# Updating the states of sample units in row tiles of TensorE

## Chip, cores and metric

One core of one Trainium2 chip runs the whole program. The metric is the time of one launch on the device, in microseconds (us).

## The reference, cut to what matters

The program computes one layer of a decoder for a prompt of 2048 tokens and for a group of 8 short sample sequences of 8 tokens each. One of its three parts is an mLSTM: per head a matrix memory C (256 x 256) and a key sum n (256), which are decayed and then given the weighted outer products of a chunk's keys and values:

```python
C_new = w_C[..., None, None] * C + jnp.einsum('bhs,bshd,bshe->bhde', w_s, kb, vb)
n_new = w_C[..., None] * n + jnp.einsum('bhs,bshd->bhd', w_s, kb)
```

For the samples there are 8 sequences x 4 heads = 32 such states, each updated once, by the 8 tokens of its sequence. All is float32.

## The kernel before, in words

The program runs in phases: the projections of all tokens, then gates, convolution and attention, and last the recurrence, `recur()`, the phase that the change touches. It goes over 16 tiles t of 128 prompt tokens. The engines have their programs written out one by one, with semaphores between them; the order on TensorE is the loop at L2175. In each tile TensorE makes

- the numerators of the four heads (L2059, L2060), into banks 1 to 4;
- eight updates of the prompt's states (L2072), for head j // 2 and half d = j % 2 of the keys: the product `kw` x `v1` has 128 x 257 elements. Column 257 of `v1` is all ones, so that the last column of the product is the key sum. The products alternate between the two banks DC = (0, 5), and VectorE adds each of them to the decayed state (L2418);
- between the updates, the output projection of the tile before, in 16 parts of three products (L2090 to L2092) into banks 6 and 7, and the turning of the next tile's values and output gates (L2107) into banks 3, 4, 1 and 2, from where ScalarE reads them (L2251, and the tanh of L2256);
- the turning of the next tile's keys into banks 1 and 2 (L2033), the scores (L2042) into bank 0, and the turning of its own outputs (L2124) into banks 3 and 4.

The sample states are worked on in eight units u, each four sequences of one head. Sequence b of a unit has its 8 tokens in partitions 32 b to 32 b + 7; the other partitions of its 32 are zero. A unit has its front (turning the keys and scores, L2142 and L2144) in an even tile and its back in the odd tile behind it: the numerators (L2157 and L2160, which put the four sequences side by side in four column tiles of 8 of 32 columns), and the update of its states. Before the change a unit has eight updates (L2075), one for each sequence b and half d. The product is over all 128 partitions: `skw[:, d, :]`, the weighted keys of all four sequences, by `sv[:, p, b, :]`, in which only the rows of sequence b aren't zero. They stand as j = 8 to 15 behind the eight updates of the prompt, each with one output part behind it. VectorE adds them to `sC` in the same way (L2418), and at the end copies the key sums from column 257 of `sC` into `nT` (L2467). Then it scales the unit's outputs (L2469), which TensorE turns (L2168).

In an odd tile VectorE's order is: first half of the prompt's and the unit's outputs, updates 0 to 7 (after the sixth of them the final norm of an earlier tile), the second half of the tile's outputs (L2430), updates 8 to 15, and the second half of the unit's outputs. SyncE stores the states of the unit of a tile in the tile after it (L1936), behind its wait for the low parts of the outputs (L2387).

A float32 product shows as two records of TensorE in the profile, each with its own weight load; it is streamed in two passes.

Of the kernel before, what the change touches and what calls it, by code (L numbers as in the profile page):

```python
# [19 lines left out]
ALU = mybir.AluOpType  # L20
# [3 lines left out]
P = 128  # L24
# [6 lines left out]
NT = T // P  # L31
H = 4
HD = 256
# [1771 lines left out]
def back_of(t):  # L1805
    return t // 2 if t > 0 and t % 2 == 1 and t // 2 < UNITS else None


def recur(nc, S, sb, bank, w, ident, raw, work, wide, acc_late, area, nT, mask, smask, columns, wmh, wml, g_final, st_C, C_prompt,
# [47 lines left out]
    def unit(u):  # L1857
        return u // 4, u % 4

    def updates_before(t):  # L1860

        return 8 * t + 8 * sum(back_of(x) is not None for x in range(t))

    def vo_bank(t, g):

# [33 lines left out]
    @block.sync  # L1899
    def _(sp):  # L1900
        def early(t):
            if t >= NT:
                return
            p, c = t % 2, slice(t * P, (t + 1) * P)
            if t >= 2:
                sp.wait_ge(S["st_summed"], t - 1)
                wait(sp, S["qs_ready"], 4 * (t - 2))
                sp.dma_start(qk[:, p, :, :], w["qk"][:, :, c].rearrange("f p t -> p f t")).then_inc(S[f"qk_loaded{p}"], 16)
                sp.wait_ge(S["nm_ready"], t - 1)
            if t >= 2:  # L1910
                load_gates(sp, w, br, t, S[f"br_loaded{p}"])

        def values(t):
            if 0 < t < NT:
                sp.wait_ge(S["vo_turned"], 4 * t)
                load_rows(sp, w, "vo", vo, t, S["vo_loaded"])

        def gates(t):
            if 0 < t < NT:
                sp.wait_ge(S["y_split"], 2 * t)  # L1920
                load_rows(sp, w, "z", z, t, S["z_loaded"])

        def residual(s):
            if s < TILES:
                p, t = s % ACC, OUTS[s]
                wait(sp, S[f"y_stored{p}"], 16 * (s // ACC))
                if t >= NT - 1:
                    sp.wait_ge(acc_late, 32)
                sp.dma_start(acc[0:width(t), p, :], w["acc"][t * P:t * P + width(t), :]).then_inc(S[f"acc_loaded{p}"], 16)

        def store_unit(u):
            (i, h), p = unit(u), u % 2
            sp.wait_ge(S["C_updated"], updates_before(2 * u + 1) + 16)
            for d in range(2):
                at = slice(d * P, (d + 1) * P)
                sp.dma_start(C_sample[0, 4 * i:4 * i + 4, h, at, :].rearrange("b p e -> p b e"),  # L1936
                             sC[:, p, :, d, 0:HD]).then_inc(S[f"s_stored{p}"], 16)

        values(1)
        sp.dma_start(swcb[:, :, :], w["wc"][H * NT:].rearrange("(h b) -> h b", h=H).partition_broadcast(P)).then_inc(S["s_gates_loaded"], 16)  # L1940
        sp.dma_start(gf[:, :], row_bcast(g_final, P)).then_inc(S["gf_loaded"], 16)
        for t in range(NT):
            early(t + 2)
            residual(t)
            if back_of(t - 1) is not None:
                store_unit(back_of(t - 1))
            values(t + 2)
            if t == 0:
                load_unit(sp, 1)
            gates(t + 1)  # L1950
            if back_of(t - 1) is not None:
                load_unit(sp, back_of(t - 1) + 2)
        residual(NT)
        sp.wait_ge(S["C_updated"], updates_before(NT))
        sp.dma_start(C_prompt[0, 0].rearrange("h (a p) e -> p h a e", p=P), C[:, :, :, 0:HD]).then_inc(S["state_stored"], 16)
        sp.dma_start(n_prompt[0, 0].rearrange("h (a p) -> p h a", p=P), C[:, :, :, HD]).then_inc(S["state_stored"], 16)
        store_unit(UNITS - 1)
        sp.wait_ge(S["s_n_out"], 1)
        sp.dma_start(n_sample[0].rearrange("b h d -> (b h) d"), nrow[:, :]).then_inc(S["state_stored"], 16)
        sp.wait_ge(S["state_stored"], 48)  # L1960
        sp.wait_ge(S["s_stored0"], 32 * 4)
        sp.wait_ge(S["s_stored1"], 32 * 4)
# [62 lines left out]
    def _(pe):  # L2025
        def turn_keys(t):
            p = t % 2
            if t >= 2:
                pe.wait_ge(S[f"qk_loaded{p}"], 16 * (t // 2))
            if t:  # L2030
                pe.wait_ge(S["th_ready"], 2 * t + 2)
            for i in range(8):
                m = pe.transpose(bank[1 + i // 4][:, (i % 4) * P:(i % 4 + 1) * P], qk[:, p, 8 + i, :], ident[:, :])  # L2033
                if i % 4 == 3:
                    m.then_inc(S["k_turned"], 1)
# [26 lines left out]
        def update(t, j):  # L2062
            wait(pe, S["C_updated"], updates_before(t) + j - 1)
            if j == 1:
                wait(pe, S["s_y_out"], 2 * units_before(t))
                if back_of(t) is not None:
                    pe.wait_ge(S["s_t1_ready"], back_of(t) + 1)
                    pe.wait_ge(S["s_den_copied"], back_of(t) + 1)
            out = bank[DC[j % 2]][:, 0:HE]
            if j < 8:  # L2070
                h, d = j // 2, j % 2
                m = pe.matmul(out, kw[:, h, d * P:(d + 1) * P], v1[t % 2][:, h, :], start=True, stop=True)  # L2072
            else:
                p, b, d = back_of(t) % 2, (j - 8) // 2, j % 2
                m = pe.matmul(out, skw[:, d, :], sv[:, p, b, :], start=True, stop=True)  # L2075
            m.then_inc(S["dC_summed"], 1)

        def out_part(s, g):

# [37 lines left out]

        def turn_y(t):
            pe.wait_ge(S["y_ready"], 4 * t + 4)
            pe.wait_ge(S["v_ready"], 2 * min(t + 1, NT - 1) + 2)  # L2120
            if front_of(t) is not None:
                pe.wait_ge(S["s_vo_ready"], front_of(t) + 1)
            for i in range(8):
                m = pe.transpose(bank[3 + i // 4][:, (i % 4) * P:(i % 4 + 1) * P],  # L2124
                                 th[t % 2][:, i * P:(i + 1) * P], ident[:, :])
                if i % 4 == 3:
                    m.then_inc(S["y_turned"], 1)

        def turn_n():
            pe.wait_ge(S["s_n_kept"], UNITS)  # L2130
            pe.wait_ge(S["s_y_out"], 2 * UNITS)
            for d in range(2):
                m = pe.transpose(bank[SPARE][:DB * H, d * P:(d + 1) * P], nT[:, d, :], ident[:, :])
            m.then_inc(S["s_n_back"], 1)
# [40 lines left out]
        for t in range(NT):  # L2175
# [2 lines left out]
            parts = list(range(16)) if t else []  # L2178
            if u is not None:
                unit_numerator(u)  # L2180
                for j in range(16):
                    update(t, j)
                    if j in (2, 4):
                        turn_vo(t + 1, j // 2 - 1)
                    for g in parts[j:j + 1]:
                        out_part(t - 1, g)
            else:
                for j in range(8):
                    update(t, j)
                    if j in (2, 4):  # L2190
                        turn_vo(t + 1, j // 2 - 1)
                    if j == 6 and front_of(t) is not None:
                        unit_turn_vo(front_of(t))
                    for g in parts[2 * j:2 * j + 2]:
                        out_part(t - 1, g)
# [146 lines left out]
    def _(dve):  # L2342
# [63 lines left out]

        def update(t, j):
            dve.wait_ge(S["dC_summed"], updates_before(t) + j + 1)
            if j < 8:
                c, decay = C[:, j // 2, j % 2, :], wcb[:, (j // 2) * NT + t:(j // 2) * NT + t + 1]  # L2410
            else:
                u, b = back_of(t), (j - 8) // 2
                i, h = unit(u)
                c, decay = sC[:, u % 2, b, j % 2, :], swcb[:, h, 4 * i + b:4 * i + b + 1]
            if t == 0:
                dve.tensor_copy(c, bank[DC[j % 2]][:, 0:HE]).then_inc(S["C_updated"], 1)
                return
# [14 lines left out]
        def n_of(u):  # L2432

            i, h = unit(u)
            return nT.ap().rearrange("p d (b h) -> p b d h", h=H)[:, 4 * i:4 * i + 4, :, h]

        def unit_weights(u):
            dve.wait_ge(*unit_loads(u))
# [21 lines left out]
        def unit_second_half(u):  # L2460
# [2 lines left out]
            dve.wait_ge(S["s_den_ready"], u + 1)  # L2463
            ch.step(dve.scalar_tensor_tensor(scoef[:, :], srden[:, :], 0.25, srinv[:, :], ALU.mult, ALU.mult))
            ch.sync()
            dve.wait_ge(S["C_updated"], updates_before(2 * u + 2))
            dve.tensor_copy(n_of(u), sC[:, p, :, :, HD]).then_inc(S["s_n_kept"], 1)  # L2467
            dve.wait_ge(S["s_t1_ready"], u + 1)
            dve.tensor_scalar(so[:, p, :], so[:, p, :], scoef[:, :], None, ALU.mult).then_inc(S["s_y_ready"], 1)  # L2469

# [12 lines left out]
        for t in range(NT):  # L2483
# [3 lines left out]
            first_half(t)  # L2487
            if u is not None:
                unit_first_half(u)
            n = 16 if u is not None else 8  # L2490
            for j in range(n):
                update(t, j)
                if j == 5 and t >= 2:
                    final_norm(t - 2)
                if j == 7:
                    second_half(t)
            if u is not None:
                unit_second_half(u)
            score_weights(t + 1)
            if front_of(t) is not None:  # L2500
# [37 lines left out]
```

## Time and profile before

| | |
|---|---|
| median of 3 runs | 2168.04 us |
| lowest and highest | 2162.81 and 2168.23 us |
| profiled execution, its time | 2160.53 us |
| its span from first to last instruction | 2158.7 us |
| TensorE busy | 2104.6 us, 97% of the span |
| VectorE, ScalarE, GpSimd busy | 64%, 44%, 42% |
| recurrence | from about 1674 us to the end |

The rows of a profile name the line of the kernel, the engine and the operation, the output and its inputs, and the shapes. PE is TensorE's matmuls and PEld its weight loads, which overlap them; DVE is VectorE, ACT ScalarE, POOL GpSimd, SP SyncE. Matmuls are pipelined: a record's duration reaches beyond the start of the next one. What a record costs in a full stream is therefore read from the distances of starts, or from the chain of waits, which counts each piece of time once.

### The profile page before, as it was taken

The numbers are of one execution on the slowest core, as the hardware profiler recorded it, in microseconds if no ns is written. First come the engines' busy times: TensorE is split into PE (matmuls) and PEld (weight loads), VectorE is DVE, ScalarE is ACT, GpSimd is POOL, SyncE is SP. The second block draws the span as 40 slices with busy tenths as digits, with TensorE's granted clock in tenths as the row PEclk, the third lists the DMA queues.
The fourth block names the chain that finished last, engine by engine and source line by source line (L and its number), as shares of the span: only waits on it lengthen the run. The fifth ranks groups of instructions, "written<-read, shape, count | busy, mean of one in ns | idle before, by whom it ended". The sixth has DMA issues, their size and how long they took to land. (4 is left out here: it accounts for less than half of the span.)

```text
span 2158.7 us, 34655 instructions
## 1 busy us (share of the span) xinstructions
PE 2104.6 (97%) x12657; PEld 1966.1 (91%) x12657; DVE 1372.3 (64%) x2164; ACT 959.5 (44%) x1982; POOL 895.9 (42%) x741
## 2 busy tenths in 40 slices
PE   7899999999999999999999999899999899999997
PEld 4899999999999999999999999888887788888885
DVE  7577776697777766977787676433453455555553
ACT  5454445545444455454544554332341444443331
POOL 2455555585555555755555555210000422222210
PEclk9999999999999999999999999999999999999999
DMA  6333334434333344434334444564364766666644
GB/s 211 121 122 122 122 122 142 132 112 127 121 119 120 121 142 137 125 123 135 122 112 122 145 134 132 165 219 148 112 200 144 208 173 188 195 179 193 197 130 88
DMA packets 344008, 311.99 MB, mean 145 GB/s; under 512 B 43121, under 2 KB 306193, under 8 KB 343841
## 3 DMA queue, kind: packets, MB, share of 16 engines
q1 hardware_dynamic: 337728, 289.79, 45.2%
q0 software_dynamic: 2912, 9.64, 1.4%
q10 hardware_dynamic: 3200, 10.36, 1.2%
q8 instruction: 102, 1.67, 0.3%
q14 instruction: 66, 0.53, 0.1%
HBM read 224.82 MB, written 84.92 MB: 143 GB/s over the span
## 5 line engine op out<-in xcount | busy, mean ns | idle before, releaser
L672 PE MATMUL bank<-xh,wh 128*128 128x352 f32 x2688 | 870.2, 324 | 10.0 <-ACT snap L844 8.3
L674 PE MATMUL bank<-xh,wl 128*128 128x352 f32 x2688 | 866.0, 322 | 0.0
L673 PE MATMUL bank<-xl,wh 128*128 128x352 f32 x2688 | 863.7, 321 | 0.0
L1025 DVE TENSOR_TENSOR wl<-raw,wh 128x512 fp32r<-128x512 f32 x384 | 417.6, 1090 | 207.7 <-ACT wh L809 206.7
L672 PEld LDWEIGHTS bank<-xh,wh 128*128 128x128 f32 x2688 | 505.1, 188 | 12.2 <-ACT snap L844 9.5
L674 PEld LDWEIGHTS bank<-xh,wl 128*128 128x128 f32 x2688 | 507.5, 189 | 0.0
L673 PEld LDWEIGHTS bank<-xl,wh 128*128 128x128 f32 x2688 | 506.4, 188 | 0.2 <-issue 0.2
L844 ACT ACTIVATE snap<-bank 128x352 f32<-128x352 f32 x384 | 178.5, 465 | 373.8 <-PE bank L674 373.8
L809 ACT ACTIVATE wh<-raw 128x512 fp32r<-128x512 f32 x384 | 241.2, 630 | 169.5 <-PE bank L674 154.5
L1025 DVE TENSOR_TENSOR wl<-wt,wh 128x512 fp32r<-128x512 f32 x288 | 237.7, 830 | 112.7 <-ACT wh L809 111.9
L620 POOL TENSOR_TENSOR stage<-snap 128x352 f32<-128x352 f32 x96 | 97.8, 1019 | 460.9 <-ACT snap L844 459.7
L809 ACT ACTIVATE wh<-wt 128x512 fp32r<-128x512 f32 x288 | 180.3, 626 | 116.1 <-PE bank L674 110.3
L604 POOL TENSOR_TENSOR wt<-raw 128x512 f32<-128x512 f32 x96 | 161.8, 1685 | 64.3 <-DMA raw<-in_w_in 49.8
L1974 POOL TENSOR_TENSOR work<-area,mask 128x512 f32<-128x512 f32 x16 | 20.4, 1274 | 391.2 <-DVE work L2357 207.3
L1043 DVE TENSOR_TENSOR stage<-bank,snap 128x352 f32<-128x352 f32 x288 | 149.4, 519 | 46.7 <-PE bank L674 41.5
L608 POOL TENSOR_TENSOR raw<-raw 128x512 f32<-128x512 f32 x96 | 164.2, 1710 | 0.0
L607 POOL TENSOR_TENSOR wt<-raw,wt 128x512 f32<-128x512 f32 x96 | 154.7, 1612 | 11.3 <-DVE wl L1025 4.0
L611 POOL TENSOR_TENSOR wt<-raw,wt 128x512 f32<-128x512 f32 x96 | 142.2, 1481 | 10.8 <-DVE wl L1025 10.8
L2090 PE MATMUL bank<-wm_h,m_yh 128*128 128x512 f32 x256 | 131.9, 515 | 0.0
L2418 DVE SCALAR_TENSOR_TENSOR m_C<-m_C,wcb,bank 128x257 f32<-128x257 f32 x120 | 57.5, 479 | 107.0 <-PE bank L2072 106.8
L2091 PE MATMUL bank<-wm_l,m_yh 128*128 128x512 f32 x256 | 101.0, 394 | 0.0
L2092 PE MATMUL bank<-wm_h,m_yl 128*128 128x512 f32 x256 | 100.9, 394 | 0.0
(308 smaller groups left out, 2765.3 us busy)
## 6 DMA issues: line engine op xcount, KB each, us to landing
raw<-in_w_in SPq DMA_DIRECT2D x72, 1024.0 KB, 5.5
raw<-in_w_in SPq DMA_DIRECT2D x48, 512.0 KB, 5.4
scr_vo<-stage SPq DMA_DIRECT2D x48, 352.0 KB, 7.0
scr_qk<-stage SPq DMA_DIRECT2D x48, 352.0 KB, 6.4
raw<-scr_qk SPq DMA_DIRECT2D x16, 1024.0 KB, 7.0
area<-scr_vo SPq DMA_DIRECT2D x16, 1024.0 KB, 9.6
scr_z<-stage SPq DMA_DIRECT2D x24, 352.0 KB, 2.2
scr_xa<-stage SPq DMA_DIRECT2D x24, 352.0 KB, 2.3
```

The costliest lines, as they stand in the source:

```text
L604: pool.tensor_tensor(wt[:, 0], b12, b11, ALU.subtract).then_inc(S["t_ready"], 1)
L607: pool.tensor_tensor(wt[:, 1], b22, wt[:, 0], ALU.subtract).then_inc(S["t_ready"], 1)
L608: pool.tensor_tensor(b12, b22, b12, ALU.subtract).then_inc(S["t_ready"], 1)
L611: pool.tensor_tensor(wt[:, 2], b21, wt[:, 1], ALU.subtract).then_inc(S["t_ready"], 1)
L672: pe.matmul(out, wh[:, b, k, :], xh[:, b, k, :], start=(first and k == 0), stop=False, skip_group_check=True)
L673: pe.matmul(out, wh[:, b, k, :], xl[:, b, k, :], start=False, stop=False, skip_group_check=True)
L674: m = pe.matmul(out, wl[:, b, k, :], xh[:, b, k, :], start=False, stop=(k == 3), skip_group_check=True)
L809: act.activation(halves(q, b)[0], source(q, b), ACT.Copy).then_inc(S["w_high"], 1)
L844: act.activation(snap[:, n, :], g if n == 1 else b, ACT.Copy).then_inc(S["snap"], 1)
L1025: dve.tensor_tensor(low, source(q, b), high.bitcast(F32), ALU.subtract).then_inc(S["w_low"], 1)
L1043: dve.tensor_tensor(out, src, snap[:, add, :], ALU.add).then_inc(S["out_dve"], 1)
L2090: pe.matmul(out, h[:, k, :], wmh[:, k, c], start=(k == 0), stop=False)
```

## The change

Each unit's eight updates over 128 partitions give way to eight products over 32 partitions each. The weights are `skw[32b:32b+32, d, :]`, the moving data the 256 value columns of sequence b in the same partitions, and each sequence b writes its own bank 1 + b, both halves d beside each other. So the four products of a half d use the four row tiles of 32 of the array, and the two halves make two rounds. The key sums of the unit become two products more, over all 128 partitions, with four columns each: column 257 of `sv` for the four sequences, into bank 0. VectorE updates the key sums in two operations of 128 x 8, and the states in four of 128 x 512, each for both halves of a sequence, straight from its bank. TensorE takes the key sums and the eight products in one go behind the eighth update of the prompt; the second half of the output parts follows without anything between. New waits on TensorE: before the rounds, that banks 1 to 4 have been read (first half of VectorE's outputs, the tanh of the next tile); before the next tile's keys are turned and before the tile's outputs are turned, that VectorE has read the four banks. The store of a unit's states waits for its four state updates; the copy of the key sums at L2467 goes.

```diff
         def update(t, j):
...
             else:
-                p, b, d = back_of(t) % 2, (j - 8) // 2, j % 2
-                m = pe.matmul(out, skw[:, d, :], sv[:, p, b, :], start=True, stop=True)
+                for d in range(2):
+                    m = pe.matmul(out[:, 4 * d:4 * d + 4], skw[:, d, :], sv[:, back_of(t) % 2, :, HD], start=True, stop=True,
+                                  skip_group_check=True)
             m.then_inc(S["dC_summed"], 1)
+
+        def unit_update(t, u):
+            pe.wait_ge(S["t1_ready"], 4 * t + 4)
+            pe.wait_ge(S["den_ready"], t + 1)
+            if t + 1 < NT:
+                pe.wait_ge(S["th_ready"], 2 * (t + 1) + 2)
+            for d in range(2):
+                for b in range(4):
+                    r = slice(32 * b, 32 * b + 32)
+                    m = pe.matmul(bank[1 + b][:, d * HD:(d + 1) * HD], skw[r, d, :], sv[r, u % 2, b, 0:HD], start=True,
+                                  stop=True, skip_group_check=True)
+            m.then_inc(S["s_dC_summed"], 1)
...
         def turn_keys(t):
...
+            wait(pe, S["s_C_updated"], 4 * units_before(t))
...
         def turn_y(t):
             pe.wait_ge(S["y_ready"], 4 * t + 4)
+            wait(pe, S["s_C_updated"], 4 * units_before(t + 1))
...
                 unit_numerator(u)
-                for j in range(16):
+                for j in range(8):
                     update(t, j)
                     if j in (2, 4):
                         turn_vo(t + 1, j // 2 - 1)
-                    for g in parts[j:j + 1]:
-                        out_part(t - 1, g)
+                    out_part(t - 1, j)
+                update(t, 8)
+                unit_update(t, u)
+                for g in range(8, 16):
+                    out_part(t - 1, g)
...
+            if j == 8:
+                (i, h), p = unit(back_of(t)), back_of(t) % 2
+                n = sC[:, p, :, :, HD]
+                ch.step(dve.tensor_tensor(n, n, swcb[:, h, 4 * i:4 * i + 4].unsqueeze(2).broadcast_to([P, 4, 2]), ALU.mult))
+                ch.sync()
+                dve.tensor_tensor(n_of(back_of(t)), n, bank[DC[0]][:, 0:8].rearrange("p (d b) -> p b d", d=2),
+                                  ALU.add).then_inc(S["C_updated"], 1)
+                return
...
+        def unit_update(u):
+            (i, h), p = unit(u), u % 2
+            dve.wait_ge(S["s_dC_summed"], u + 1)
+            for b in range(4):
+                c = sC[:, p, b, :, 0:HD]
+                dve.scalar_tensor_tensor(c, c, swcb[:, h, 4 * i + b:4 * i + b + 1],
+                                         bank[1 + b].ap().rearrange("p (d e) -> p d e", d=2), ALU.mult,
+                                         ALU.add).then_inc(S["s_C_updated"], 1)
```

## Rows read from the trace of the kernel before

**Rows 1.** Head of the page: span, busy time by engine, granted TensorE clock.

```profile
span 2158.7 us, 34655 instructions
...
PE 2104.6 (97%) x12657; PEld 1966.1 (91%) x12657; DVE 1372.3 (64%) x2164; ACT 959.5 (44%) x1982; POOL 895.9 (42%) x741
...
PEclk9999999999999999999999999999999999999999
```

**Rows 2.** Table of windows, the recurrence between its start and its tail.

```profile
core 0: us, PE busy (x) PEld busy (x) DVE busy (x) ACT busy (x) POOL busy (x), PEclk, DMA share, GB/s
1687.00:2122.00 435.00, 430.93 (x2464) 366.84 (x2464) 242.92 (x644) 171.16 (x438) 109.00 (x167) 1.00 0.62 177
```

**Rows 3.** Waits in the recurrence: who waited for what, us, times, longest.

```profile
PE bank L2107 <- DMA area<-scr_vo: 4.8, 1, 4.8
...
PEld bank L2072 <- issue: 3.5, 8, 0.4
PEld bank L2157 <- issue: 2.7, 8, 0.3
```

**Rows 4.** Chain of waits in an odd tile: start us, us, what.

```profile
1831.91 0.43 PE bank L2075 x2
1832.34 0.23 PE bank L2090
...
1833.04 0.43 PE bank L2075 x2
...
1839.80 0.43 PE bank L2075 x2
...
1840.92 0.87 PE bank L2033 x8
```

**Rows 5.** Chain of waits around the numerators of the same tile.

```profile
1819.07 0.43 PE bank L2060 x2
1819.50 0.98 PE bank L2157 x16
1820.49 0.43 PE bank L2160 x8
1820.92 0.63 PE bank L2072 x2
```

**Rows 6.** Chain of waits, scores and a unit's front in an even tile.

```profile
1867.60 1.79 PE bank L2042 x16
1869.39 0.22 PE bank L2142 x2
1869.61 0.37 PE bank L2144 x4
```

**Rows 7.** Timeline of VectorE in the odd tile of rows 4.

```profile
1831.84 1.14 DVE L2430 TENSOR_SCALAR m_wide<-m_wide,m_coef 128x256 f32<-128x256 f32 x4
1832.89 1.10 DVE L2418 SCALAR_TENSOR_TENSOR m_s_C<-m_s_C,m_wide,bank 128x257 f32<-128x257 f32 x2
...
1840.27 0.48 DVE L2418 SCALAR_TENSOR_TENSOR m_s_C<-m_s_C,m_wide,bank 128x257 f32<-128x257 f32 x1 [0.65 <-PE bank L2075]
1840.67 0.16 DVE L2464 SCALAR_TENSOR_TENSOR m_s_coef<-m_s_rden,m_s_rinv 128x1 f32<-128x1 f32 x1
1840.86 0.18 DVE L2467 COPY nT<-m_s_C 128x8 f32<-128x8 f32 x1
```

**Rows 8.** Timeline of ScalarE in that tile, the two tanh.

```profile
1827.47 1.08 ACT L2256 ACTIVATE area<-bank 128x512 f32<-128x512 f32 x2 [2.02 <-PE bank L2107]
```

**Rows 9.** Groups of VectorE by line and shape, from a bank.

```profile
L2381 DVE TENSOR_TENSOR area<-bank,area 128x512 f32<-128x512 f32 x30 | 19.2, 681 | 0.0
...
L2357 DVE SCALAR_TENSOR_TENSOR work<-bank,work 128x512 f32<-128x512 f32 x15 | 10.4, 692 | 34.5 <-issue 34.5
```

**Rows 10.** Timeline of TensorE at the end of the last tile.

```profile
2122.44 0.44 PE L2168 MATMUL bank<-ident,m_s_o 128*128 128x128 f32 x2 [0.41 <-DVE m_s_o L2469]
```

**Rows 11.** Waits of SyncE's queue in the recurrence.

```profile
SPq L1314 <- DVE m_yl L2387: 225.1, 14, 23.4
```

More of the change, by code:

```diff
@@ L1860, in updates_before @@
     def updates_before(t):
-        return 8 * t + 8 * sum(back_of(x) is not None for x in range(t))
+        return 8 * t + units_before(t)
     def vo_bank(t, g):
@@ L1932, in store_unit @@
             (i, h), p = unit(u), u % 2
-            sp.wait_ge(S["C_updated"], updates_before(2 * u + 1) + 16)
+            sp.wait_ge(S["s_C_updated"], 4 * (u + 1))
             for d in range(2):
@@ L2129, in turn_n @@
         def turn_n():
-            pe.wait_ge(S["s_n_kept"], UNITS)
+            pe.wait_ge(S["C_updated"], updates_before(NT))
             pe.wait_ge(S["s_y_out"], 2 * UNITS)
@@ L2408, in update @@
             dve.wait_ge(S["dC_summed"], updates_before(t) + j + 1)
[L2409 to L2414, printed above, removed]
+            if j == 8:
[6 more added lines that the diff above has]
+                return
+            c, decay = C[:, j // 2, j % 2, :], wcb[:, (j // 2) * NT + t:(j // 2) * NT + t + 1]
             if t == 0:
@@ L2465, in unit_second_half @@
             ch.sync()
-            dve.wait_ge(S["C_updated"], updates_before(2 * u + 2))
-            dve.tensor_copy(n_of(u), sC[:, p, :, :, HD]).then_inc(S["s_n_kept"], 1)
             dve.wait_ge(S["s_t1_ready"], u + 1)
@@ L2489, in _ @@
                 unit_first_half(u)
-            n = 16 if u is not None else 8
-            for j in range(n):
+            for j in range(8):
                 update(t, j)
@@ L2494, in _ @@
                     final_norm(t - 2)
-                if j == 7:
-                    second_half(t)
+            second_half(t)
             if u is not None:
+                update(t, 8)
+                unit_update(u)
                 unit_second_half(u)
```

## The prediction

> **What bounds the kernel now.** I read the page first. TensorE is busy for 97% of the span at an unthrottled clock, VectorE for 64% [rows 1]. Cut into stages, the table of windows shows that the recurrence, the only stage that the change touches, has TensorE busy for 430.93 of 435.00 us at a granted clock of 1.00 (the 2.4 GHz level), VectorE for 243 and ScalarE for 171 [rows 2]. The waits of the recurrence say what the last 4 us are: one wait for a load of vo at its start, before the first sample unit is updated [rows 3]. Nothing else holds TensorE for long, so here the time is the length of TensorE's instruction stream, and a matmul taken out of it is taken out of the end, as long as no other engine comes to be waited for.
>
> The chain of waits shows the eight updates of a sample unit standing on that path in the odd tile that begins near 1818 us: an update (two records, since a float32 product is streamed in two passes) takes 0.43 us, the three products of an output part 0.70 us, and the pattern repeats until the keys of the next tile are turned at 1840.92 [rows 4]. This is repeated in each of the eight odd tiles.
>
> **What is removed.** Eight updates, 8 x 0.43 = 3.44 us of TensorE per unit. Nothing hides them: the output parts beside them are TensorE's too.
>
> **What is added on TensorE.** Four costs per unit.
>
> 1. The rounds. Eight products of 32 rows and 256 columns, two passes each, are 16 records. If the four row tiles run side by side, a round costs what one product does, two passes of 0.215, so two rounds cost 0.86 us. No product of this trace uses row tiles 1 to 3, so this has to be bounded. The nearest rows are the unit's numerators, which use the array's four column tiles of 32: 16 records of 257 columns take 0.98 us on the chain and 8 more take 0.43, where two such records at full width take 0.43 [rows 5]. So 8 float32 records took the time of 2: the four tiles ran side by side, in both passes. Upper end: nothing runs side by side, 16 x 0.215 = 3.44 us. I take 0.86, because row and column tiles are the same split turned round, each row tile here has its own partitions to read and its own bank to write, and the column tiles show that the passes of float32 are no obstacle.
>
> 2. Change of the array's shape. Going into the numerators, the first 16 records take 0.98 us instead of twice 0.43: 0.11 lost. Coming out, the first full product takes 0.63 instead of 0.43: 0.20 lost [rows 5]. The weight loads stand idle at just these two places, eight times each [rows 3]: after a change of shape the first weights aren't loaded ahead. The way out loads 128 columns first and the way in only 8, so I put the difference of 0.1 to the width of the load. The new unit has 128 columns on either side, 0.20 twice: 0.40 us per unit. Ends: nothing (if row tiles need no such change) to 0.80 (twice).
>
> 3. The key sums. They used to ride along as column 257 at the price of one column; now they are two products of four columns with full 128 x 128 weights. The nearest rows are two products of 32 columns: four records take 0.37 us on the chain, hardly less a record than the score products of 128 columns, 16 in 1.79 us or 0.11 each [rows 6]. A quarter of the columns at nearly the same price: the loads of 128 columns of weights set it, not the columns. I take 4 x 0.11 = 0.44 us. Ends: nothing (all hidden) to 0.86 (two full updates).
>
> The Trainium skill (TensorEngine Tiling, Instruction Overhead) says that a matmul of one column costs what one of 60 does, about 60 cycles; by that the key sums would be about 0.1 us and the whole change 2.7 us better than my sum. The records of 32 columns took 0.09 us each, so I go by them.
>
> 4. Three more waits ahead of the rounds, for work that is long done: the second tanh of the next tile has ended by 1828.6 [rows 8], the rounds start after 1832.3. VectorE's first half ended before the updates did. Nothing.
>
> Sum per unit: 0.86 + 0.40 + 0.44 = 1.70 against 3.44, so 1.74 us less, and 8 x 1.74 = 13.9 us.
>
> The Trainium skill (TensorE: Matmul & The Clock Gate, Measured speedup vs the span model) gives 3.07x for four row tiles of 32 with 512 columns. By that the rounds would be 3.44 / 3.07 = 1.12 us and the whole gain 11.8 us instead of 13.9; the column tiles' rows here show almost the full fourfold.
>
> **What moves on VectorE, and the new wait.** Before, it made 8 updates of 0.48 us, the last one right behind TensorE, at 1840.27 [rows 7]. Now it makes two 128 x 8 operations (the copy of the key sums, of the same size, takes 0.18 [rows 7]) and four of 128 x 512 from a bank (0.69 each by the nearest two rows [rows 9]). TensorE now waits for these four before it turns the next keys into banks 1 and 2; behind that wait stand the scores, the next numerators and all the rest of TensorE's stream. When does it bite? VectorE is free of the second half at 1831.84 + 1.14 = 1832.98 [rows 7], makes the key sums until about 1833.4, has the banks from about 1833.6 and is done by 1833.6 + 4 x 0.69 = 1836.4. TensorE, after the rounds, has 8 x 0.70 = 5.6 us of output parts and comes to the wait at 1840.92 - 1.74 = 1839.2. Slack 2.8 us, so nothing. It would take 1.4 us for each operation to use it up.
>
> **Small gains and transfers.** In the last tile no keys are turned, and TensorE waits 0.41 us for the sample output that VectorE scales after the last update [rows 10]; now VectorE is done 2 us earlier: 0.4 us off, once. The store of the states can't start earlier than now, since SyncE stands at its wait for the tile's low parts most of the time (225.1 us in 14 waits [rows 11]) and comes to the store only in the next tile; that is no loss either. Loads of vo, z and keys are issued at points of TensorE's stream and are needed a tile later, so they lose 1.7 us of some 20.
>
> **Result of the sum.** 13.9 + 0.4 = 14.3 us. The profiled execution took 2160.53 us, so it would take 2146.2. The median of the runs shown is 2168.04, 7.5 us above the profiled one; there the same gain gives 2153.7 us, which is what I predict.
>
> **Rivals.**
>
> *Rounds overlap only in part.* Each of the 16 records brings 128 columns of weights where the numerators' brought 8, and the score products show one such load in 0.11 us, one after another [rows 6]. If the four row tiles can't load at the same time, the rounds take 16 x 0.11 = 1.78 us. (Were the two passes of a tile to hold back the next tile, it would be nine passes, 1.94.) Per unit 3.44 - (1.78 + 0.40 + 0.44) = 0.82 less, 6.6 + 0.4 = 7.0 us in all: 2161.0. For it: nothing in the trace shows two loads of 128 columns at once. Against it: each row tile loads from other partitions. The Trainium skill (TensorE: Matmul & The Clock Gate, LDWEIGHTS) speaks for it in so far as it says that a load of 32 rows takes as long as one of 128; whether four such loads overlap, no run here shows.
>
> *Nothing overlaps (slower).* If row tiles that write all 128 partitions of four banks must take turns, the rounds cost what the updates did, and the shape change and the key sums come on top: 8 x 0.84 = 6.7, less 0.4, is 6.3 us more: 2174.3. It turns to a loss once the 16 records take more than 2.6 us, 0.16 each. Against it: the column tiles' rows [rows 5].
>
> *The new wait on VectorE bites.* If VectorE ended more than 2.8 us later than worked out, TensorE would stall in eight tiles, 8 us for each further us. At the durations of the rows it doesn't come near. A transfer that becomes late I hold for as unlikely.
>
> **How the numbers follow.** A measurement of this kernel can tell about 0.3%, 6.5 us, from no change. Side by side: 0.66, 2153.7 us; its own range, with shape change and key sums at their ends together, is 2147.5 to 2160. In part: 0.22, 2161.0, three quarters of it faster by over 0.3%. Nothing: 0.07, 2174.3, half of it beyond 0.3%. A new wait or a late transfer that eats much of the gain: 0.05. So faster 0.81, same 0.14, slower 0.05. The range must take in the lower end of the first case and most of the second: 2147 to 2163.
>
> **What would show it.** In the profile after: in each odd tile one group of 16 records with 32 rows, some 0.9 us from its first start to the next group's (1.8 in the second case, 3.4 in the third); a gap of about 0.1 us and an exposed weight load on either side; four records of four columns over 0.44 us; eight output parts in a row at 0.70; no idle time of TensorE before the turn of the keys; odd tiles 1.7 us shorter than before, even tiles the same. The prediction is wrong if the group of 16 is much longer, or if TensorE stands before the keys.

## The result

The changed kernel takes 2147.44 us in the median of 4 runs (2145.6 to 2152.09), the kernel before 2167.1 us (2162.81 to 2168.23, 4 runs). The ratio is 0.9921, with a 95% interval of 0.9904 to 0.9938. The profiled executions took 2147.59 and 2160.53 us, with spans of 2145.8 and 2158.7.

The profile after, in the chain of waits of the odd tile that answers to [rows 4] and [rows 5] (start us, us, what; the keys of a tile are turned at L2034 now):

```profile
1808.78 0.87 PE bank L2034 x8
...
1818.14 0.98 PE bank L2172 x16
1819.13 0.43 PE bank L2175 x8
1819.56 0.63 PE bank L2073 x2
...
1830.55 0.34 PE bank L2076 x4
1830.89 1.08 PE bank L2088 x16
1831.97 0.43 PE bank L2104
1832.40 0.23 PE bank L2105
...
1837.76 0.87 PE bank L2034 x8
```

And of the kernel before, the turn of the keys with which the tile of [rows 4] begins (its end, at 1840.92 us, stands in [rows 4]):

```profile
1810.14 0.87 PE bank L2033 x8
```

The length of an odd tile, from one turn of the keys to the next, is 1840.92 - 1810.14 = 30.78 us before and 1837.76 - 1808.78 = 28.98 us after. The 16 records of the rounds (L2088) take 1.08 us, the key sums (L2076) 0.34 us, and the output product behind them 0.43 instead of 0.23 us: 1.62 us in place of 3.44. The numerators before them are unchanged to 0.01 us. Even tiles take 25.8 us in both kernels. Read in this way, the lengths of the odd tiles repeat to 0.02 us and those of the even ones to 0.05 us within each of these kernels, which makes them the sharpest measure for the experiments. The first tile and the last differ from one execution to the next.

VectorE in the same tile, timeline after, beside [rows 7]:

```profile
1830.48 1.14 DVE L2451 TENSOR_SCALAR m_wide<-m_wide,m_coef 128x256 f32<-128x256 f32 x4
1831.53 0.17 DVE L2430 TENSOR_TENSOR m_s_C<-m_s_C,m_wide 128x8 f32<-128x8 f32 x1
1831.73 0.17 DVE L2432 TENSOR_TENSOR nT<-m_s_C,bank 128x8 f32<-128x8 f32 x1
1832.04 2.72 DVE L2463 SCALAR_TENSOR_TENSOR m_s_C<-m_s_C,m_wide,bank 128x512 f32<-128x512 f32 x4
```

Its four operations end at 1832.04 + 2.72 = 1834.76, and TensorE comes to the keys at 1837.59 (its record; the chain counts 0.17 later). So 2.8 us of slack are left, and no wait of TensorE for these operations stands in the list. The list of waits in the recurrence has the changes of shape, eight each (who waited for what: us, times, longest); L2104, the first output product behind the rounds, is new beside [rows 3]:

```profile
PEld bank L2073 <- issue: 3.5, 8, 0.4
...
PEld bank L2172 <- issue: 2.7, 8, 0.3
PEld bank L2104 <- issue: 2.7, 8, 0.3
```

In the last tile the wait of [rows 10] for the sample output is gone, as the timeline after shows. Its second line is a later stall of that tile, for VectorE, which both kernels have:

```profile
2109.61 0.38 PE L2183 MATMUL bank<-ident,m_s_o 128*128 128x128 f32 x2
...
2114.65 0.66 PE L2104 MATMUL bank<-wm_h,m_s_yh 128*64 128x512 f32 x1 [3.56 <-DVE m_wide L2384]
```

The stretch from the last turn of keys to TensorE's last record is 55.69 us instead of 58.17, 1.82 for the rounds and 0.66 for this wait and what hung on it. (By the starts of the records the wait had cost 0.58 us and not the listed 0.41, since a record's duration reaches into it.) Seven odd tiles of 1.81 and the 2.48 of the last one make 15.2 us. The spans differ by only 12.9: in this execution the recurrence began 2.86 us later than in the one before, of which its first tile gave 0.56 back. The two kernels are the same up to there.

TensorE at the start of the recurrence in the timeline after:

```profile
1677.34 1.94 PE L2034 MATMUL bank<-ident,raw 128*128 128x128 f32 x8 [3.28 <-PEq L64]
```

and in the kernel before:

```profile
1674.48 1.94 PE L2033 MATMUL bank<-ident,raw 128*128 128x128 f32 x8 [3.29 <-PEq L64]
```

### The profile page after: what moved, and what is told of

Its sections match the earlier page's. It is cut to its first block and busy times, and to the rows that moved or that the text cites. A ratio compares the mean times of both kernels' runs of the same rounds, so it can differ in the third digit from the quotient of the medians.

```text
span 2145.8 us, 34710 instructions
## 1 busy us (share of the span) xinstructions
PE 2093.5 (98%) x12689; PEld 1954.2 (91%) x12689; DVE 1363.7 (64%) x2140; ACT 959.3 (45%) x1982; POOL 896.2 (42%) x741
## 5 line engine op out<-in xcount | busy, mean ns | idle before, releaser
L607 POOL TENSOR_TENSOR wt<-raw,wt 128x512 f32<-128x512 f32 x96 | 154.7, 1612 | 11.3 <-DVE wl L1025 4.1
L2104 PE MATMUL bank<-wm_h,m_yh 128*128 128x512 f32 x256 | 120.8, 472 | 0.0
```

Of the source, the lines that this page charges most:

```text
L607: pool.tensor_tensor(wt[:, 1], b22, wt[:, 0], ALU.subtract).then_inc(S["t_ready"], 1)
L2104: pe.matmul(out, h[:, k, :], wmh[:, k, c], start=(k == 0), stop=False)
```

## The experiments

**The changed kernel timed again** (`after_again`). No edit.

> The changed kernel once more, timed in five rounds. If the gain is only what the recurrence shows in the profile (1.82 us in each of eight odd tiles and 0.6 us in the last, 15.2 us in all), the time is 15.2 us below the kernel before, ratio 0.9930. If the change also takes time out of what lies ahead of the recurrence or around the span, the ratio stays near the 0.9909 of the two medians.

Measured: 2147.51 us (5 runs) against 2163.22 (15 runs), ratio 0.9920, interval 0.9902 to 0.9938. Odd tiles 28.97 us, even ones 25.78, as in the first profile. The interval holds both 0.9930 and 0.9909, so the times can't tell the 4.5 us between the two. The two medians here lie 15.7 us apart, close to the 15.2. The profiles show where such differences can come from: the spans of the two profiles of the same code, 2145.8 and 2140.5 us, differ by 5.3 us, and none of it is in the odd tiles. The recurrence began 2.34 us earlier, at 1675.00, its first tile was 1.47 us shorter, and the last one 1.41 us, since there the clock stayed at 2.4 GHz behind the stall of 3.56 us (granted clock 1.00 in the 3 us behind it, 0.50 in the first profile). Over the twelve profiles of this study, all of which have the same program up to that point, it began between 1674.48 and 1682.38 us.

**The same products without row tiles** (`full_rows`).

```diff
-                    r = slice(32 * b, 32 * b + 32)
+                    r = slice(0, P)
```

> The same eight products, banks, order and waits, but each over all 128 partitions (the rows of the other sequences are zero, so that the result is the same). If the gain is the four row tiles running side by side, the rounds cost 8 x 0.43 = 3.44 us, there is no change of shape, and an odd tile takes 28.97 - 1.08 - 0.20 + 3.44 = 31.13 us, 0.34 us more than before the change; time 2 us above the kernel before. If the gain came from putting the updates in one go, or from VectorE's fewer operations, an odd tile stays near 29 us and the time well below the kernel before.

Measured: 2167.43 us (10 runs) against 2163.22, ratio 1.0015 (1.0004 to 1.0026). The chain of this kernel:

```profile
1814.89 0.87 PE bank L2034 x8
...
1836.66 0.34 PE bank L2076 x4
1837.01 3.57 PE bank L2088 x16
1840.57 0.23 PE bank L2104
...
1846.16 0.87 PE bank L2034 x8
```

An odd tile takes 31.27 us, 0.5 more than before the change, where 0.34 were expected. One slice apart, the same 16 records take 3.57 or 1.08 us. The whole gain in the odd tiles is the four row tiles side by side; everything else in the change (the order, the separate key sums, VectorE's fewer operations) costs 0.5 us per unit. The 0.13 us over 3.44 stands in front of the rounds: behind a key sum's record of four columns the next record starts 0.11 us later, here the first of the rounds as well, so that the load of its 128 columns of weights isn't hidden. The output product behind is back at 0.23, so that the 0.20 there belongs to the change of shape.

**Row tiles of 64** (`rows_of_64`).

```diff
-                for b in range(4):
-                    r = slice(32 * b, 32 * b + 32)
+                for b in (0, 2, 1, 3):
+                    r = slice(64 * (b // 2), 64 * (b // 2) + 64)
```

> Each product over 64 partitions (the half that holds its sequence; the rest is zero), in the order of sequences 0, 2, 1, 3, so that two row tiles of 64 can run side by side. If time goes by how many tiles run at once, the rounds take 8 / 2 x 0.43 = 1.72 us and 0.2 for the change of shape, and an odd tile 28.97 + 0.86 = 29.83 us. If the shape itself decides and not the number, 28.97 (all overlap) or 31.3 us (none do).

Measured: odd tiles 29.83 us, as expected to the hundredth; time 2155.52 us in one run. (A single run says little here, since the start of the recurrence alone moves by up to 7.9 us from one execution to another, as the last section says. In all runs below that were made once, the tiles decide.) The chain has the rounds at

```profile
1833.76 1.93 PE bank L2088 x16
```

Rounds of 3.57, 1.93 and 1.08 us for one, two and four tiles at once: one pass of 0.215 us for each group of records that fits side by side (16, 8 and 4 passes), and to get in 0.13 us without row tiles and 0.21 and 0.22 with them. A pass here is one record; with 256 columns in 0.215 us at a granted clock of 1.00 (2.4 GHz) it takes two periods of the clock for a column.

**Both halves of a sequence one after the other** (`halves_inside`).

```diff
-            for d in range(2):
-                for b in range(4):
+            for b in range(4):
+                for d in range(2):
```

> The same eight products in another order: both halves of sequence 0, then of sequence 1, and so on. If each row tile has a stream of its own that runs ahead of the others, an odd tile stays at 28.97 us. If products start strictly in the order of the program, so that one waiting for its own tile holds back those behind it, the four tiles hardly overlap: 13 passes of 0.215 instead of 4, 1.9 us more, odd tile 30.9 us.

Measured: odd tiles 28.99 us, rounds 1.10 us in the chain; 2147.99 us in one run. The order makes a difference of 0.02 us: a tile that is busy with its first product doesn't hold back the products of the others behind it. The first four records of the group start within 0.04 us of each other; the records don't name their row tile, but in the strict order of the program only the first of them could start then. The nine passes that a strict order would take in the change, and the thirteen here, don't occur.

**An output part between the rounds** (`split_rounds`).

```diff
                                   stop=True, skip_group_check=True)
+                if d == 0:
+                    out_part(t - 1, 8)
...
-                for g in range(8, 16):
+                for g in range(9, 16):
```

> One output part (128 rows) between the two rounds, so that the shape of the array changes four times a unit instead of twice. If a change of shape costs 0.20 us on either side, an odd tile takes 28.97 + 0.40 = 29.37 us. If the 0.4 us beside the rounds have another cause (the start of a group, the waits ahead of it), it stays at 28.97 us.

Measured: odd tiles 29.38 us; 2154.70 us in one run. The chain:

```profile
1833.85 0.34 PE bank L2076 x4
1834.19 0.65 PE bank L2088 x8
...
1835.73 0.65 PE bank L2088 x8
```

Each round is now two passes, 0.43, and 0.22 for the way in. A change of shape costs about 0.2 us in each direction, so two pairs of them cost 0.8 us a unit.

**Without the unit's key sums** (`no_key_sums`).

```diff
-                update(t, 8)
                 unit_update(t, u)
...
             second_half(t)
             if u is not None:
-                update(t, 8)
                 unit_update(u)
```

The second part is VectorE's program, which leaves out its two operations for the key sums; the count of updates that the waits go by is lowered to match.

> The unit's key sums are left out on TensorE and on VectorE (the sample key sums that come out are then the old ones); everything else stays. If the chain's 0.34 us is their price, an odd tile takes 28.63 us; by 0.11 us for each of four loads of 128 columns of weights, 28.53. If they lie hidden, 28.97.

Measured: odd tiles 28.64 us, rounds 1.08 us as before; 2151.18 us in one run, in which the recurrence began later than in any other, at 1682.38 us. The key sums cost 0.33 us a unit, 2.6 us in all. Four loads of 0.11 would be 0.44, but the first is hidden behind the 512 columns of the output product in front of it: in the profile after, the four records of the key sums start 0.03, 0.11 and 0.11 us apart. With the output product in front of the rounds the way in still costs 0.22, so the load that the key sums leave exposed (the 0.13 us of `full_rows`) isn't paid on top of the change of shape. That the two are one and the same load is the simplest reading of this, and isn't shown by itself.

**The rounds later in the tile** (`rounds_after_12`, `rounds_after_14`, `rounds_last`). The edit puts key sums and rounds behind the 12th, the 14th or the 16th output part; for the 12th:

```diff
+                for g in range(8, 12):
+                    out_part(t - 1, g)
                 update(t, 8)
                 unit_update(t, u)
-                for g in range(8, 16):
+                for g in range(12, 16):
                     out_part(t - 1, g)
```

> Key sums and rounds behind the twelfth output part: four parts, 2.8 us, are left to cover VectorE, which ends 2.8 us after the rounds. If the cover needed is just VectorE's four operations, an odd tile stays at 28.97 us or loses a tenth or two. If more hangs behind them (the unit's outputs, the scores), it loses clearly more.

> Key sums and rounds behind the last output part instead of ahead of the ninth. Nothing then covers VectorE's four operations, which end 2.8 us after the rounds: TensorE stands at the turn of the next keys for about 2.8 us in each odd tile, an odd tile takes 31.8 us, and the time is about 8 us above the kernel before. If the wait on VectorE does not matter (or the banks are handed on one by one), an odd tile stays at 28.97 us and the time 15 us below.

> Key sums and rounds behind the fourteenth output part: 1.4 us of output parts are left to cover VectorE's 2.8. In the kernel with the rounds last, a stall of 2.94 us was followed by products at half the clock, and the time rose by 22 us instead of the 8 expected. If the stall alone is paid here, TensorE stands for about 1.5 us, an odd tile takes 30.5 us, an even tile 25.8, all at full clock. If any stall brings the clock down, the even tiles grow too, as they did with the rounds last (25.8 to 28.4 us).

Measured, from the starts of the tiles in the timelines:

| rounds behind part | odd tile, us | even tiles, us | stall before the keys, us |
|---|---|---|---|
| 8 (the change) | 28.97 | 25.8 | 0 |
| 12 | 29.08 | 25.8 | none listed |
| 14 | 30.48 | 25.8 | 1.4 |
| 16 | 31.88 | 25.8 to 28.4 | 2.9 |

The cover that the new wait needs is VectorE's four operations, 2.7 us, that is four output parts. With less, TensorE stands for what is missing: 1.4 us for two parts too few, 2.9 for four. In single runs `rounds_after_12` took 2150.83 us and `rounds_after_14` 2162.39. So far the expectations held. But with the rounds last the time is 2185.86 us (4 runs), ratio 1.0098 (1.0079 to 1.0117), some 22 us above the kernel before where 8 were expected. The timeline of TensorE there shows where most of the rest is:

```profile
1904.73 1.15 PE L2088 MATMUL bank<-m_s_v,work 32*128 32x256 f32 x16
1908.81 1.94 PE L2034 MATMUL bank<-ident,raw 128*128 128x128 f32 x8 [2.94 <-DVE m_s_C L2463]
```

The turn of the keys takes 1.94 us where the same eight products take 1.04 in the kernels before and after. The windows of that stretch (us, busy of PE, PEld, DVE, ACT, POOL, then the granted clock, DMA share, GB/s) show what goes with it:

```profile
1905.90:1908.81 2.91, 0.00 (x1) 0.03 (x1) 2.83 (x6) 0.00 (x0) 0.00 (x0) 0.77 0.33 100
1908.81:1913.95 5.14, 5.14 (x24) 5.14 (x25) 0.31 (x1) 1.63 (x4) 0.00 (x0) 0.50 0.00 0
1914.34:1918.69 4.35, 4.35 (x26) 3.91 (x25) 4.19 (x8) 2.34 (x6) 2.91 (x3) 1.00 0.30 119
```

Within the 2.9 us without a product the granted clock falls (0.77 on average), it is at 1.2 GHz for the keys and the scores, and back at 2.4 GHz for the numerators. The even tiles behind six of the seven stalls are 1.3 to 2.6 us longer for it, 11.3 us in all, beside the 7.7 us that the odd tiles have over the kernel before. The last tile adds 1.8 us: TensorE waits 3.30 us there for the sample output. With stalls of 1.4 us the even tiles stay at 25.8.

**The rounds last, with the banks handed on one by one** (`last_by_bank`). Key sums and rounds stand as in `rounds_last`. The turn of the keys waits for the first of VectorE's four operations before bank 1 and for the second before bank 2.

```diff
-            wait(pe, S["s_C_updated"], 4 * units_before(t))
             for i in range(8):
+                if units_before(t) and i % 4 == 0:
+                    pe.wait_ge(S["s_C_updated"], 4 * units_before(t) - 3 + i // 4)
```

> Rounds last again, but the turn of the next keys waits for each of its two banks alone: for VectorE's first operation before bank 1, for its second before bank 2; the turn of the outputs still waits for all four. If the long stall is the cause of both the wait and the fall of the clock, the stall shrinks to about 0.9 us (the first operation behind the rounds) and some 0.2 before bank 2, an odd tile takes about 30.1 us, and even tiles stay at 25.8. If the four operations as a whole bind anyway, through the turn of the outputs or the scores, an odd tile stays near 31.9.

Measured: odd tiles 29.91 us, even ones 25.97, the 0.17 between them and 25.8 being the second wait; time 2165.59 us in one run, 2162.96 for the kernel before beside it. The list of waits (us in total, times, longest) has

```profile
PE bank L2035 <- DVE m_s_C L2464: 6.7, 7, 1.0
```

against this in the kernel with the rounds last and one wait for all four:

```profile
PE bank L2034 <- DVE m_s_C L2463: 20.6, 7, 2.9
```

So 1.8 of the 2.9 us of that stall (1.97 in the odd tile, less the 0.17 that come back) were waits that the turn of the keys didn't need where it stood: for banks 3 and 4, which it doesn't use, and for bank 2 ahead of its turn. Behind the seven stalls that are left the granted clock stays at 1.00. Where the rounds stand in the change, the coarse wait costs nothing.

## Why the prediction was right

**What bounds.** Right. All that was taken from TensorE's stream in an odd tile came off the tile: 1.82 us of work gone, 1.82 us shorter.

**The rounds, 0.86 us.** Right. With the way in they are 1.08, and `split_rounds`, `rows_of_64` and `full_rows` fit two passes of 0.215 for each round. The bound of 3.44 for no overlap is what `full_rows` shows with the same instructions. Reading row tiles off column tiles [rows 5] was the step with the most risk in it. The rival that 128 columns of weights can't be loaded into four tiles at once was wrong by the rounds' length: 0.86 us and not 1.78 beside the way in, 1.08 with it. The records of the loads are as long for one row tile as for a full one (ns, min/median/max), and they run beside each other: the first four of a group start 0.007 us apart, where the full loads of the key sums follow each other after 0.11 us.

```profile
L2088 PEld LDWEIGHTS bank<-m_s_v,work x128: 181/184/185, 1721.3 to 2103.4; 32*128 32x128 f32 x128
```

By the Trainium skill (TensorE: Matmul & The Clock Gate, LDWEIGHTS), a load of 32 rows takes as long as one of 128; the trace agrees, 184 ns against the 188 ns of the records it replaced. The 3.07x that the Trainium skill gives for four row tiles with 512 columns (TensorE: Matmul & The Clock Gate, Measured speedup vs the span model) was too low for the place where I set it against the rounds alone, with 256 columns: 3.44 / 0.86 is fourfold. With both changes of shape it is 3.44 / 1.28 = 2.7.

**The change of shape, 0.40 us.** Right: 0.22 in and 0.20 out. I had worked it out from two rows, a way in with 8 columns to load first and a way out with 128, and `split_rounds` bears it out (0.41 for a second pair). On the way in, 0.13 of the 0.22 would be there without a change of shape, behind the key sums (`full_rows`). That the difference of 0.1 us between ways in with 8 and with 128 columns is the width of the load fits the 0.22 here, but no run varies the width alone.

**The key sums, 0.44 us.** Right in kind, 0.1 too large: 0.34 in the chain, 0.33 when they are left out. I counted four exposed loads; the first hides behind a long product. That is where the sum's miss per unit comes from.

**VectorE and the new wait.** Right. Worked out: done at 1836.4 for a turn of keys at 1839.2, slack 2.8 us; measured 2.8. The series of positions shows that the wait is real and that the place of the rounds decides over it. My price for this rival was 8 us for each further microsecond. For a stall of 1.4 us it was about right: seven odd tiles grew by 1.51 us each, and in the last, which turns no keys, TensorE waits 1.72 us for the sample output instead. It was too low for one of 2.9 us, since I left the clock out of it.

**The last tile, 0.4 us.** 0.66 in the pair of profiles. The idle time of 0.41 that I read in [rows 10] is counted from the modelled end of a record; by the starts the wait was 0.58.

**The sum.** 13.9 + 0.4 = 14.3 us predicted, 15.2 in the profile: 0.08 us too little for each unit, and 0.3 in the last tile. The median came out at 2147.4 and not 2153.7, mainly because I took the gain off a median of 2168.04, of three runs, while the median of the 15 later runs of the same kernel is 2163.22: that base is 4.8 of the 6.3 us, the sum's miss 0.9. Off the later median the same sum gives 2148.9. So it was luck that the time still lies in the range of 2147 to 2163, 0.4 us above its lower end: the range was set for the terms of the sum, and it was the base that was off. The range that I gave the first case by itself is also misadded at its lower end: with 0.84 us less in each of eight units it begins at 2147.0 and not at 2147.5. Of the ratio's 0.9920, or 17 us, the profile explains 15.2 (the medians of that comparison differ by 15.7); the interval holds that, and whether the rest is anything stays open.

## What to carry to other kernels

Where products fill only 32 of 128 rows because the rest are zeros, cutting them into row tiles with a bank each runs four in the time of one, float32 included, in either of the two orders tried; but each entry into and exit from the shape cost some 0.2 us here, so gather all such products in one go. A result that used to ride along as an extra column isn't free once it stands alone: it pays its weight loads. And put the group where enough other TensorE work follows to cover the engine that empties the banks; what is missing is paid in full, and behind stalls of 2.9 us it was paid a second time in six of seven cases, through the clock.

## What the runs showed of the hardware that was not expected

A stall of 2.9 us on TensorE was followed in six of seven cases by products at 1.2 GHz, in two of them with the keys and scores at a granted clock of 0.50 from first to last, in the others for a part of them; stalls of 1.0 and 1.4 us, seven of each, were not. In the last tile ten of the twelve profiles have a stall of 3.56 us, and behind nine of them the granted clock was below 1.00 in the next 3 us. The tenth is `after_again`, whose last tile is 1.4 us shorter than in the first profile of the same kernel. So the last tile's length carries a part that comes and goes.

The time ahead of the recurrence, the same program in all twelve profiles, varies by 7.9 us from one execution to another, and the first tile, with its wait for a load, takes between 19.9 and 24.7 us. The odd tiles repeat to 0.02 us within a kernel. In a kernel like this a gain of 2 us is read from tile lengths, and not from the time of the launch.
